# Hybrid streaming encoder step on one core: the prompt tiles' state-times-keys product moved into level 6, the output product reordered, and the gate-projection fillers dealt anew

## The chip, the cores and the metric

The kernel runs on one core of one Trainium2 chip. The metric is the device time of one execution in microseconds (us); the median of three runs is given. The engines are PE (TensorE, matrix products), DVE (VectorE), ACT (ScalarE), POOL (GpSimd) and SP (SyncE, which issues most transfers). Each works through its own instructions in the order in which they are written; between engines only semaphores order the work.

## What is computed

Two macaron layers on a residual stream of width 1024, for 512 prompt tokens and 8 sample groups of 16 tokens that share all weights. The first layer's mixer has four gated-DeltaNet heads and four mLSTM heads of size 128. The change touches the DeltaNet heads on the prompt alone:

```python
def gated_delta_chunked(q, k, v, beta, g, S0):
    ...
    A = jnp.eye(cs, dtype=jnp.float32) + jnp.where(strict, beta[..., :, None] * kk * gam, 0.0)
    eG = jnp.exp(G)
    rhs = jnp.concatenate([beta[..., None] * v, (beta * eG)[..., None] * k], axis=-1)
    sol = lax.linalg.triangular_solve(A, rhs, left_side=True, lower=True, unit_diagonal=True)
    u_v, w = sol[..., :dv], sol[..., dv:]
    p_qk = jnp.einsum('nbhtd,nbhsd->nbhts', q, k) * gam
    k_end = k * jnp.exp(G[..., -1:] - G)[..., None]
    def step(S, xs):
        q_c, u_v_c, w_c, p_c, eG_c, k_end_c, gL_c = xs
        u = u_v_c - jnp.einsum('bhtk,bhkv->bhtv', w_c, S)
        o = eG_c[..., None] * jnp.einsum('bhtk,bhkv->bhtv', q_c, S) + jnp.einsum('bhts,bhsv->bhtv', p_c, u)
        S = jnp.exp(gL_c)[..., None, None] * S + jnp.einsum('bhsk,bhsv->bhkv', k_end_c, u)
        return S, o
```

The kernel computes u as the inverse of A times (beta v minus the state times beta e^G k), so the inverse and that difference are independent of each other until the product u.

## The kernel before, in words

The program is a list of stages; the one that matters is `core`, some 170 us of the span, between the input projection and the output projection of the even mixer. It works through four prompt tiles of 128 tokens (`delta_tile`, t = 0 to 3) and then the sample tile. Nothing schedules it: the order on each engine is written out by hand. W(0) to W(8) are SBUF tiles of 128 x 4 heads x 128 floats, bank(i) is a PSUM bank, and heads(i) is the same bank seen as four heads.

A prompt tile on PE, in order: the product of keys and beta keys (`kk`); the second half of the last tile's mLSTM update (`up1`); 24 filler products; keys times queries (`np`); 4 fillers; then levels 1 to 6 of the inversion of A by doubling. A level is: two half products `m1` (two heads each), a copy of each half by ACT to W(8) (`m1c`), at level 5 a product `d2`, then two half products `d`, which DVE subtracts from W(7) (semaphore `xr`, L2838). In levels 1 to 4 DVE also transposes the half into W(6) (`x6`, L2841), and the next level's `m1` halves wait for that. At the end of each level DVE also makes the next level's mask product W(1) (`masked`, L2791, semaphore `ctl`). Between these stand parts of the mLSTM heads (`mlstm_part`) and fillers.

Behind level 6 come: `ks`, the state pS times W(0), the decayed beta keys, for which PE waits for the last `xr`; DVE's difference W(6) = v minus that (L2870, semaphore `rT`); PE's four transposes of it (L1427), ACT's copy (L2395, `rtok`), PE's product `u`, ACT's copy of it to W(1) (L2400, `utok`), and PE's output products: per head W(1) times W(5) (L1438), which waits for `utok`, and the state times q (L1439), then the state's own update and, on DVE, `keep_state`.

DVE, behind L2870, goes on with `beta_products` of the next tile (L2798 and L2580), the mLSTM denominators (L3102, a maximum of two SBUF tiles, and L3103, a reciprocal), `gate_columns`, the mLSTM output, `keep_state`, and `delta_head` of the next tile, whose product L2817 writes G_b: the first `m1` of the next tile waits for it. `kk` of the next tile waits for `gate_columns` (`expin`).

The fillers (`z_fill`, L1350) are the projection of eight weight blocks of 1024 x 128 on the tokens, 384 products of 128 x 320 in 16 halves of 24. The tables Z_FIRST, Z_HEAD, Z_D, Z_NEXT, Z_KS and Z_RT say how many stand at each place. The first product of a block waits for the low part of that block's weights (`lo_ready`), which POOL makes (L1064) after ACT's cast (`prep`, L1863). Six blocks are prepared inside the tiles: block 3, 5, 7 behind ACT's copy L2395 of tiles 0, 1, 2, and block 4, 6, 8 at level 4 of tiles 1, 2, 3. DVE also scales finished halves (`z_scale`, L2788).

```python
        Z_FIRST = 48
        Z_HEAD, Z_KS, Z_RT = 4, 8, 6
        Z_D = {1: 0, 2: 2, 3: 0, 4: 3, 5: 6, 6: 6}
        Z_NEXT = {1: 7, 2: 2, 3: 8, 4: 4, 5: 2, 6: 2}
```

Of the kernel before, what the change touches and what calls it, by code (L numbers as in the profile page):

```python
# [5 lines left out]
def stream_step(nc, ins, outs):  # L6
# [44 lines left out]
    with ctx:  # L51
# [148 lines left out]
        def bank(i):  # L200
            return ps[i // 2][:, i % 2, :]
# [69 lines left out]
        def half_at(t, l, g):  # L271

            return 2 * ((LVL - 1) * t + l - 1) + g + 1
# [21 lines left out]
        def V(i):  # L295
# [109 lines left out]
            "prod", "expin", "c0", "x0", "xt0",  # L405
            "gam", "eg",
            "kk", "np", "np_read", "tr", "ktr",
            "kend", "ctl", "x6", "xr",
            "m1", "d2", "d", "ks",
            "m1c", "rtok", "utok",  # L410
            "rT", "rt", "u", "o",
# [2 lines left out]


        Z_FIRST = 48
        Z_HEAD, Z_KS, Z_RT = 4, 8, 6
        Z_D = {1: 0, 2: 2, 3: 0, 4: 3, 5: 6, 6: 6}
        Z_NEXT = {1: 7, 2: 2, 3: 8, 4: 4, 5: 2, 6: 2}
        Z_BANK = [5, 2, 5, 5, 4, 0, 5, 4, 5, 5, 5, 4, 0, 5, 4, 5]  # L420

        def z_before(half):
# [665 lines left out]
        def _(pe):  # L1088
# [266 lines left out]
            def delta_tile(s, filled, t):  # L1355
                L = LVL
                q, k = qkv[:, 0:HA, tile(t)], qkv[:, HA:2 * HA, tile(t)]
                li, l2 = (LVL - 1) * t, (LVL - 2) * t
                if t == 0:
                    token_rows(0)  # L1360
                    z_fill(s, filled, Z_FIRST)

                pe.wait_ge(core["prod"], t + 1)

                pe.wait_ge(core["expin"], t + 1)
                per_head(4, lambda h: k[:, h], lambda h: W(0)[:, h]).then_inc(core["kk"], 1)
                if t:
                    mlstm_part(t - 1, "up1")
                z_fill(s, filled, 24)

                if t:

                    pe.wait_ge(core["up"], t)
                per_head(3, lambda h: k[:, h], lambda h: q[:, h]).then_inc(core["np"], 1)
                z_fill(s, filled, Z_HEAD)

                for l in range(1, L):
                    pe.wait_ge(core["ctl"], li + l)
                    if l == 1:

                        pe.wait_ge(core["x0"], t + 1)
                        if t % 2:

                            pe.wait_ge(z_out, Z_AT_LEVEL[t])
                    for g in range(2):
                        if l > 1:

                            pe.wait_ge(core["x6"], x6_at(t, l - 1, g))

                            pe.wait_ge(core["xr"], half_at(t, l - 1, g))  # L1390
                        c_l = G_b if l == 1 else W(1)
                        per_head(g, lambda h: c_l[:, h], lambda h: W(6)[:, h], which=TWO[g]).then_inc(core["m1"], 1)
                    if l == 1:

                        pe.wait_ge(core["xt0"], t + 1)

                        pe.wait_ge(core["np_read"], t + 1)
                        for h in range(HA):
                            last = pe.transpose(bank(3)[:, h * P:(h + 1) * P], k[:, h], ident[:])
                        last.then_inc(core["ktr"], 1)  # L1400

                    if l == 4:
                        mlstm_part(t, "kt")
                    z_fill(s, filled, Z_D[l])

                    if l < L - 1 and not quad_level(l):

                        pe.wait_ge(core["m1c"], half_at(t, l, 1))
                        per_head(2, lambda h: W(7)[:, h], lambda h: W(8)[:, h]).then_inc(core["d2"], 1)
                    for g in range(2):  # L1410

                        pe.wait_ge(core["m1c"], half_at(t, l, g))
                        per_head(g, lambda h: W(8)[:, h], lambda h: W(7)[:, h], which=TWO[g]).then_inc(core["d"], 1)

                    for part in {2: ["qk"], 3: ["vt", "kin"], 4: ["num"], 5: ["den"], 6: ["up0"]}.get(l, []):
                        mlstm_part(t, part)
                    z_fill(s, filled, Z_NEXT[l])

                pe.wait_ge(core["xr"], half_at(t, L - 1, 1))
                per_head(3, lambda h: pS[:, h], lambda h: W(0)[:, h]).then_inc(core["ks"], 1)  # L1420
                z_fill(s, filled, Z_KS)

                pe.wait_ge(core["rT"], t + 1)

                pe.wait_ge(z_out, Z_AT_RT[t])
                for h in range(HA):
                    last = pe.transpose(bank(4)[:, h * P:(h + 1) * P], W(6)[:, h], ident[:])  # L1427
                last.then_inc(core["rt"], 1)
                z_fill(s, filled, Z_RT)

                pe.wait_ge(core["rtok"], t + 1)
                per_head(3, lambda h: W(7)[:, h], lambda h: W(8)[:, h]).then_inc(core["u"], 1)

                token_rows(t + 1)

                pe.wait_ge(core["utok"], t + 1)
                for h in range(HA):
                    pe.matmul(bank(2)[:, h * P:(h + 1) * P], W(1)[:, h], W(5)[:, h], start=True, stop=False)  # L1438
                    pe.matmul(bank(2)[:, h * P:(h + 1) * P], pS[:, h], q[:, h], start=False, stop=True)  # L1439
                per_head(3, lambda h: W(3)[:, h], lambda h: W(1)[:, h]).then_inc(core["o"], 1)  # L1440
                if t == NTILE - 2:
                    mlstm_part(t, "up1")
# [396 lines left out]
        def _(act):  # L1839
# [207 lines left out]
            for s in stages:  # L2047
# [263 lines left out]
                elif kind == "core":  # L2311
# [46 lines left out]
                    for t in range(NTILE - 1):  # L2358
                        L = LVL
                        li, l2 = (LVL - 1) * t, (LVL - 2) * t  # L2360
                        decays(t)
                        if t == 0:
                            z_copy(1)
                            prep(z0 + 2)
                        z_copy([2, 5, 9, 12][t])
                        for l in range(1, L):

                            for g in range(2):

                                act.wait_ge(core["m1"], half_at(t, l, g))  # L2370
                                act.copy(two(W(8), g), two(heads(g), g)).then_inc(core["m1c"], 1)
                            for part in {2: ["gates", "qin"], 3: ["floor", "vt", "kin"], 4: ["kt"], 6: ["den"]}.get(l, []):
                                mlstm_part(t, part)
                            if l == 1:

                                act.wait_ge(core["eg"], t + 1)
                                load_beta_G(t + 1)
                                if t:

                                    act.wait_ge(ml_dve, ml(ML_DVE, t - 1, "out"))  # L2380
                                    load_floor(t)
                            z_now = {(0, 4): 3, (1, 3): 6, (1, 6): 7, (2, 4): 10, (3, 3): 13, (3, 6): 14}
                            if (t, l) in z_now:
                                z_copy(z_now[t, l])
                            if l == 4 and t < NTILE - 2:

                                act.wait_ge(ml_dve, ml(ML_DVE, t, "qk"))
                                load_gates(t + 1)
                            if l == 4 and t:
                                prep(z0 + [4, 6, 8][t - 1])  # L2390
                        if t % 2 == 0:
                            z_copy((4, 11)[t // 2])

                        act.wait_ge(core["rt"], t + 1)
                        act.copy(W(8), heads(4)).then_inc(core["rtok"], 1)  # L2395
                        if t < NTILE - 2:
                            prep(z0 + [3, 5, 7][t])

                        act.wait_ge(core["u"], t + 1)
                        act.copy(W(1), heads(3)).then_inc(core["utok"], 1)  # L2400
                        if t % 2:
                            z_copy((8, 15)[t // 2])
# [170 lines left out]
        def _(dve):  # L2573
# [277 lines left out]
            def delta_tile(t):  # L2851
# [4 lines left out]
                    beta_products(0)  # L2856
                delta_head(t)
                for l in range(1, LVL):
                    delta_level(t, l, LVL)

                    for part in {2: ["qk"], 3: ["q"]}.get(l, []):
                        mlstm_part(t, part)
                    if l == 5:
                        mul(W(0), W(0), W(2))
                        mul(q, q, W(2))
                    for half in Z_SCALE.get((t, l), []):
                        z_scale(half)

                dve.wait_ge(core["ks"], t + 1)
                own(dve.tensor_tensor(W(6), v, heads(3), ALU.subtract).then_inc(core["rT"], 1), core["rT"])  # L2870
                if t < NTILE - 2:
                    beta_products(t + 1)
                mlstm_part(t, "scale")
# [798 lines left out]
```

## Time and profile before

| what | value |
|---|---|
| median of 3 runs | 2603.61 us (2600.45 to 2605.82) |
| the profiled execution's own time | 2603.56 us |
| its span, first to last instruction | 2601.8 us |
| mean granted TensorE clock | 0.996 of full speed |
| PE busy | 2563.9 us (99%) |
| DVE busy | 2108.2 us (81%) |
| ACT busy | 1212.5 us (47%) |
| POOL busy | 355.3 us (14%) |
| prompt tiles, from the first filler to the last tile's output products | 635.1 to 806.2 us |

The profile is of one execution. What lies around its span is 1.8 us. Matrix products overlap in the array: a product's recorded time reaches past the start of the next, so the spacing of starts tells what one costs, and the idle time that a row gives counts from the end of the record, some 0.16 us after the array could have taken the next one. The clock is at its full level throughout the core stage (1.00 in all its windows).

### The profile page before, as it was taken

The page shows a single profiled execution, that of the slowest core. Times are in us where ns is not written, and L with a number is a line of the kernel's source. Part 1 is how long each engine was busy: PE and PEld are TensorE (multiplying, and loading weights), DVE is VectorE, ACT ScalarE, POOL GpSimd, SP SyncE. Part 2 cuts the span into 40 slices and gives each one's busy share as a digit, 9 for nine tenths or more (in the row PEclk, how much of TensorE's full clock was granted, in tenths as well). Part 3 has the DMA queues.
Part 4 walks back from the last instruction along what each step waited for, and adds up shares of the span by engine and source line. Part 5 has one row for each costly group of instructions (what it writes and reads, how often), then busy time and mean ns, then how long its engine had stood idle before and what let it go on. Part 6 is the DMA issues. An engine that isn't in the chain of part 4 may idle for free.

```text
span 2601.8 us, 43707 instructions
## 1 busy us (share of the span) xinstructions
PE 2563.9 (99%) x17600; PEld 2531.2 (97%) x17600; DVE 2108.2 (81%) x2614; ACT 1212.5 (47%) x1921; POOL 355.3 (14%) x186
## 2 busy tenths in 40 slices
PE   9999999999999999999999999999999999999998
PEld 9999999999999799999999999999999999999998
DVE  7979786888887789898877998987757788898756
ACT  5535454343444445454445554545311355454445
POOL 2200003232010120000023200000333300000042
PEclk9999999999999999999999999999999999999999
DMA  4223323232214422232223222322322222332231
GB/s 127 82 82 91 88 78 86 64 79 78 60 42 107 139 65 82 82 96 83 82 74 92 74 82 82 93 85 82 92 74 75 66 73 82 92 88 82 85 96 49
DMA packets 420251, 215.13 MB, mean 83 GB/s; under 512 B 19218, under 2 KB 418011, under 8 KB 420048
## 3 DMA queue, kind: packets, MB, share of 16 engines
q1 hardware_dynamic: 406066, 205.36, 27.7%
q10 hardware_dynamic: 13982, 6.96, 1.0%
q8 instruction: 140, 2.29, 0.4%
q14 instruction: 63, 0.52, 0.1%
HBM read 204.58 MB, written 7.68 MB: 82 GB/s over the span
## 4 chain that ended last, share of the span: by engine, by line
PE 83%; DVE 13%; ACT 2%; issue 1%; DMA 0%; POOL 0%; DVEq 0%; SPq 0%; ACTq 0%
PE ps L1131 16%; PE ps L1132 16%; PE ps L1133 16%; PE ps L1116 7%; PE ps L1120 7%; PE ps L1117 7%; PE ps L1326 2%; PE ps L1189 2%; PE ps L1190 2%; PE ps L1191 2%; DVE sumsq L2685 1%; DVE r L2771 1%; PE ps L1350 1%; DVE ut L2580 1%; DVE tau_lo L2649 1%
## 5 line engine op out<-in xcount | busy, mean ns | idle before, releaser
L1064 POOL TENSOR_TENSOR wlo<-raw,whi 128x1024 fp32r<-128x1024 f32 (+2 forms) x150 | 339.8, 2267 | 2208.3 <-ACT whi L1863 2208.3
L1131 PE MATMUL ps<-tau_hi,whi 128*128 128x320 f32 x1280 | 396.3, 310 | 0.5 <-ACT sq L2101 0.5
L1132 PE MATMUL ps<-tau_lo,whi 128*128 128x320 f32 x1280 | 396.0, 309 | 0.0
L1133 PE MATMUL ps<-tau_hi,wlo 128*128 128x320 f32 x1280 | 396.0, 309 | 0.0
L1874 ACT CAST whi<-raw 128x512 fp32r<-128x512 f32 (+4 forms) x368 | 258.0, 714 | 194.2 <-PE ps L1133 188.3
L1116 PE MATMUL ps<-xh,whi 128*128 128x320 f32 x1040 | 317.0, 313 | 4.3 <-POOL wlo L1064 2.3
L1117 PE MATMUL ps<-xl,whi 128*128 128x320 f32 x1040 | 313.0, 309 | 0.0
L2596 DVE TENSOR_TENSOR wlo<-raw,whi 128x512 fp32r<-128x512 f32 (+4 forms) x368 | 289.3, 800 | 17.3 <-ACT whi L1874 17.1
L1116 PE MATMUL ps<-hh,whi 128*128 128x320 f32 x928 | 281.7, 311 | 3.9 <-DVE hl L3034 1.6
L1117 PE MATMUL ps<-hl,whi 128*128 128x320 f32 x928 | 279.3, 309 | 0.0
L2596 DVE TENSOR_TENSOR wlo<-wsum,whi 128x1536 fp32r<-128x1536 f32 (+2 forms) x112 | 180.8, 1614 | 81.9 <-ACT whi L1874 80.4
L1131 PEld LDWEIGHTS ps<-tau_hi,whi 128*128 128x128 f32 x1280 | 240.8, 188 | 1.1 <-ACT sq L2101 1.0
L1132 PEld LDWEIGHTS ps<-tau_lo,whi 128*128 128x128 f32 x1280 | 240.8, 188 | 0.0
L1133 PEld LDWEIGHTS ps<-tau_hi,wlo 128*128 128x128 f32 x1280 | 240.7, 188 | 0.0
L1120 PE MATMUL ps<-xh,wlo 128*128 128x320 f32 x1040 | 236.9, 309 | 0.0
L1131 PE MATMUL ps<-xh,whi 128*128 128x320 f32 x724 | 224.2, 310 | 3.4 <-DVEq L2584 2.9
L1132 PE MATMUL ps<-xl,whi 128*128 128x320 f32 x724 | 223.8, 309 | 0.0
L1133 PE MATMUL ps<-xh,wlo 128*128 128x320 f32 x724 | 223.7, 309 | 0.0
L1131 PE MATMUL ps<-hh,whi 128*128 128x320 f32 x716 | 221.5, 309 | 0.9 <-DVEq L2584 0.6
L1132 PE MATMUL ps<-hl,whi 128*128 128x320 f32 x716 | 221.2, 309 | 0.0
L1133 PE MATMUL ps<-hh,wlo 128*128 128x320 f32 x716 | 221.1, 309 | 0.0
L1863 ACT CAST whi<-raw 128x1024 fp32r<-128x1024 f32 (+2 forms) x152 | 141.0, 929 | 160.1 <-PE ps L1120 150.6
(498 smaller groups left out, 6116.9 us busy)
## 6 DMA issues: line engine op xcount, KB each, us to landing
raw<-in_ffn_w_gu SPq DMA_DIRECT2D x320, 256.0 KB, 3.7
raw<-in_ffn_w_d SPq DMA_DIRECT2D x96, 192.0 KB, 3.0
raw<-in_w_in_even SPq DMA_DIRECT2D x32, 512.0 KB, 4.1
raw<-in_ffn_w_d SPq DMA_DIRECT2D x32, 384.0 KB, 3.6
raw<-in_w_in_odd SPq DMA_DIRECT2D x24, 512.0 KB, 3.8
raw<-in_ffn_w_gu SPq DMA_DIRECT2D x16, 512.0 KB, 4.1
raw<-in_ffn_w_d SPq DMA_DIRECT2D x64, 128.0 KB, 2.6
raw<-in_w_ple_gate SPq DMA_DIRECT2D x16, 512.0 KB, 4.0
```

What stands on the lines that cost most here:

```text
L1064: pool.tensor_tensor(ring(wlo, n), raw[:, slot, 0:kt, :], ring(whi, n).bitcast(fp32), ALU.subtract).then_inc(lo_ready, 1)
L1116: pe.matmul(ps[j % 4][:, c, 0:HT], wh[:, k], hi[:, k, cs], start=(k == 0), stop=False)
L1117: pe.matmul(ps[j % 4][:, c, 0:HT], wh[:, k], lo[:, k, cs], start=False, stop=False)
L1120: last = pe.matmul(ps[j % 4][:, c, 0:HT], wl[:, k], hi[:, k, cs], start=False, stop=(k == kt - 1))
L1131: pe.matmul(out, whi[:, w], hi(i), start=(start and i == 0), stop=False, skip_group_check=True)
L1132: pe.matmul(out, whi[:, w], lo(i), start=False, stop=False, skip_group_check=True)
L1133: last = pe.matmul(out, wlo[:, w], hi(i), start=False, stop=(i == kt - 1), skip_group_check=True)
L1189: pe.matmul(out, whi[:, w], high[:, k, cs], start=(start and k == ks[0]), stop=False, skip_group_check=True)
L1190: pe.matmul(out, whi[:, w], low[:, k, cs], start=False, stop=False, skip_group_check=True)
L1863: act.copy(ring(whi, n), raw[:, raw_pos["block", n], 0:kt, :]).then_inc(hi_ready, 1)
L1874: act.copy(group_ring(whi, p, g), group_raw(p, g)).then_inc(pair_hi, 1)
L2596: dve.tensor_tensor(group_ring(wlo, p, g), group_raw(p, g), group_ring(whi, p, g).bitcast(fp32), ALU.subtract).then_inc(pair_lo, 1)
```

## The change

In the prompt tiles, and there alone: `ks` moves from behind level 6 to the middle of level 6, behind its `m1` halves, and waits for a new semaphore `kdec`, which DVE's decayed beta keys give at level 5. DVE's difference (`rT`) moves ahead of level 6's subtractions. PE's transposes of it follow level 6's `d` at once, the mLSTM part `up0` stands behind them, and one run of 12 fillers in the place of two of 8 and 6. ACT's copy of the transposes goes to W(4), which is free by then, and not to W(8). The state-times-q products stand ahead of the wait for `utok`. Of the fillers behind the `m1` of level 6 there were 22 a tile (6, 2, 8 and 6) and are 12; of the 10 others, three stand at the end of level 1, two pairs between the `m1` halves of levels 2 and 3, one behind the `m1` of level 4, and one at each of the two places of level 5. There are 384 as before, and no other instruction is added or dropped.

```diff
-            "kend", "ctl", "x6", "xr",
+            "kdec", "ctl", "x6", "xr",
...
-        Z_HEAD, Z_KS, Z_RT = 4, 8, 6
-        Z_D = {1: 0, 2: 2, 3: 0, 4: 3, 5: 6, 6: 6}
-        Z_NEXT = {1: 7, 2: 2, 3: 8, 4: 4, 5: 2, 6: 2}
+        Z_HEAD, Z_RT = 4, 12
+        Z_PAIR = {2: 2, 3: 2}
+        Z_D = {1: 0, 2: 2, 3: 0, 4: 4, 5: 7, 6: 0}
+        Z_NEXT = {1: 10, 2: 2, 3: 8, 4: 4, 5: 3}
...
                     for g in range(2):
+                        if g:
+                            z_fill(s, filled, Z_PAIR.get(l, 0))
...
+                    if l == L - 1:
+
+                        pe.wait_ge(core["kdec"], t + 1)
+                        per_head(3, lambda h: pS[:, h], lambda h: W(0)[:, h]).then_inc(core["ks"], 1)
                     z_fill(s, filled, Z_D[l])
...
-                    for part in {2: ["qk"], 3: ["vt", "kin"], 4: ["num"], 5: ["den"], 6: ["up0"]}.get(l, []):
+                    for part in {2: ["qk"], 3: ["vt", "kin"], 4: ["num"], 5: ["den"]}.get(l, []):
                         mlstm_part(t, part)
-                    z_fill(s, filled, Z_NEXT[l])
-
-                pe.wait_ge(core["xr"], half_at(t, L - 1, 1))
-                per_head(3, lambda h: pS[:, h], lambda h: W(0)[:, h]).then_inc(core["ks"], 1)
-                z_fill(s, filled, Z_KS)
+                    if l < L - 1:
+                        z_fill(s, filled, Z_NEXT[l])
...
                 last.then_inc(core["rt"], 1)
+                mlstm_part(t, "up0")
+
+                pe.wait_ge(core["xr"], half_at(t, L - 1, 1))
                 z_fill(s, filled, Z_RT)
 
                 pe.wait_ge(core["rtok"], t + 1)
-                per_head(3, lambda h: W(7)[:, h], lambda h: W(8)[:, h]).then_inc(core["u"], 1)
+                per_head(3, lambda h: W(7)[:, h], lambda h: W(4)[:, h]).then_inc(core["u"], 1)
 
                 token_rows(t + 1)
+
+                for h in range(HA):
+                    pe.matmul(bank(2)[:, h * P:(h + 1) * P], pS[:, h], q[:, h], start=(h == 0), stop=False, skip_group_check=True)
 
                 pe.wait_ge(core["utok"], t + 1)
                 for h in range(HA):
-                    pe.matmul(bank(2)[:, h * P:(h + 1) * P], W(1)[:, h], W(5)[:, h], start=True, stop=False)
-                    pe.matmul(bank(2)[:, h * P:(h + 1) * P], pS[:, h], q[:, h], start=False, stop=True)
+                    pe.matmul(bank(2)[:, h * P:(h + 1) * P], W(1)[:, h], W(5)[:, h], start=False, stop=(h == HA - 1), skip_group_check=True)
...
-                        act.copy(W(8), heads(4)).then_inc(core["rtok"], 1)
+                        act.copy(W(4), heads(4)).then_inc(core["rtok"], 1)
...
                 for l in range(1, LVL):
+                    if l == LVL - 1:
+
+                        dve.wait_ge(core["ks"], t + 1)
+                        own(dve.tensor_tensor(W(6), v, heads(3), ALU.subtract).then_inc(core["rT"], 1), core["rT"])
                     delta_level(t, l, LVL)
...
                     if l == 5:
-                        mul(W(0), W(0), W(2))
+                        own(dve.tensor_tensor(W(0), W(0), W(2), ALU.mult).then_inc(core["kdec"], 1), core["kdec"])
                         mul(q, q, W(2))
...
-                dve.wait_ge(core["ks"], t + 1)
-                own(dve.tensor_tensor(W(6), v, heads(3), ALU.subtract).then_inc(core["rT"], 1), core["rT"])
```

The order on DVE around level 6 (the end of level 5 is the product W_92<-W_92; L2838, in the change L2847, are the two subtractions of level 6; L2870, in the change L2871, is the difference; L2798, in the change L2807, is the first beta product). Before:

```order
L2580 TENSOR_TENSOR W_92<-W_92 128x512 [waits core_xr]
L2580 TENSOR_TENSOR qkv<-qkv,W_92 128x4x128 [waits dve_own]
L2788 TENSOR_TENSOR qkv<-qkv,r 128x4x80 [waits z_out,dve_own]
L2838 TENSOR_TENSOR W_92<-W_92,ps 128x256 [waits core_d,z_scaled]
L2838 TENSOR_TENSOR W_92<-W_92,ps 128x256 [waits core_d,core_xr]
L2870 TENSOR_TENSOR W_92<-qkv,ps 128x512 [waits core_ks,core_xr]
L2798 TENSOR_TENSOR W_92<-qkv,beta_b 128x512 [waits beta_G_loaded,core_rT]
L2580 TENSOR_TENSOR qkv<-qkv,beta_b 128x4x128 [waits core_prod]
L3102 TENSOR_TENSOR V_79<-V_79 128x512 [waits ml_act,dve_own]
```

And in the change:

```order
L2877 TENSOR_TENSOR W_92<-W_92 128x512 [waits core_xr]
L2589 TENSOR_TENSOR qkv<-qkv,W_92 128x4x128 [waits core_kdec]
L2797 TENSOR_TENSOR qkv<-qkv,r 128x4x80 [waits z_out,dve_own]
L2871 TENSOR_TENSOR W_92<-qkv,ps 128x512 [waits core_ks,z_scaled]
L2847 TENSOR_TENSOR W_92<-W_92,ps 128x256 [waits core_d,core_rT]
L2847 TENSOR_TENSOR W_92<-W_92,ps 128x256 [waits core_d,core_xr]
L2807 TENSOR_TENSOR W_92<-qkv,beta_b 128x512 [waits beta_G_loaded,core_xr]
L2589 TENSOR_TENSOR qkv<-qkv,beta_b 128x4x128 [waits core_prod]
L3113 TENSOR_TENSOR V_79<-V_79 128x512 [waits ml_act,dve_own]
```

The difference stands ahead of level 6's two subtractions and not behind them; all else keeps its place.

The order on PE in tile 1, level 4, behind the mLSTM part `num` (the pairs L1690 and L1691, in the change L1699 and L1700), where four fillers stand ahead of level 5's first `m1` half. Before:

```order
L1691 MATMUL ps<-qkv,pC 128x128
L1350 MATMUL ps<-xh,wlo 128x320
L1350 MATMUL ps<-xh,whi 128x320
L1350 MATMUL ps<-xl,whi 128x320
L1350 MATMUL ps<-xh,wlo 128x320
L1326 MATMUL ps<-W_92 128x128 [waits core_xr,core_x6,core_ctl]
```

And in the change:

```order
L1700 MATMUL ps<-qkv,pC 128x128
L1351 MATMUL ps<-xl,whi 128x320
L1351 MATMUL ps<-xh,wlo 128x320
L1351 MATMUL ps<-xh,whi 128x320 [waits z_out,lo_ready]
L1351 MATMUL ps<-xl,whi 128x320
L1327 MATMUL ps<-W_92 128x128 [waits core_xr,core_x6,core_ctl]
```

The first filler of block 4, with its wait for the block's low part, stood one level later, behind the mLSTM part `den` of level 5, and is now the third of these four.

The order on PE from the middle of level 6 on, in the change (L1327 with pS is `ks`, the next four rows' products of W_92 are `d`, L1431 are the transposes, L1673 is `up0`):

```order
L1327 MATMUL ps<-W_92,pS 128x128 [waits core_kdec]
L1327 MATMUL ps<-W_92,pS 128x128 x3
L1327 MATMUL ps<-W_92 128x128 [waits core_m1c]
L1327 MATMUL ps<-W_92 128x128
L1327 MATMUL ps<-W_92 128x128 [waits core_m1c]
L1327 MATMUL ps<-W_92 128x128
L1431 MATMUL ps<-ident,W_92 128x128 [waits z_out,core_rT]
L1431 MATMUL ps<-ident,W_92 128x128 x3
L1673 MATMUL ps<-V_79 128x129 [waits ml_act]
L1673 MATMUL ps<-V_79 128x129
L1351 MATMUL ps<-xh,whi 128x320 [waits core_xr]
```

Before, six fillers stood between `m1` and `d`, two more and `up0` between `d` and `ks`, and eight between `ks` and the transposes; no filler stands between any of these now.

## Rows read from the trace of the kernel before

**Rows 1.** The page: each engine's busy time, share of the span, instructions.
```profile
PE 2563.9 (99%) x17600; PEld 2531.2 (97%) x17600; DVE 2108.2 (81%) x2614; ACT 1212.5 (47%) x1921; POOL 355.3 (14%) x186
```
**Rows 2.** PE's waits, 630 to 803 us: total us, times, longest us.
```profile
PE ps L1326 <- DVE W L2841: 2.9, 11, 0.4
PE ps L1438 <- ACT W L2400: 1.7, 3, 0.6
```
**Rows 3.** Busy time, one stretch: length; PE, PEld, DVE, ACT, POOL busy; clock, DMA.
```profile
717.17:730.42 13.25, 12.68 (x100) 12.15 (x98) 12.63 (x19) 6.21 (x13) 2.35 (x1) 1.00 0.13 40
```
**Rows 4.** Timeline of PE from tile 1's level 6 (start us, us, operation).
```profile
712.48 1.05 PE L1326 MATMUL ps<-W 128*128 128x128 f32 x8
...
714.25 1.05 PE L1326 MATMUL ps<-W 128*128 128x128 f32 x8
715.14 0.61 PE L1664 MATMUL ps<-V 128*128 128x129 f32 x4
...
715.90 1.16 PE L1326 MATMUL ps<-W,pS 128*128 128x128 f32 x8
...
718.06 0.60 PE L1427 MATMUL ps<-ident,W 128*128 128x128 f32 x4
...
720.33 0.27 PE L1331 MATMUL ps<-ident,R 128*128 128x128 f32 x1
721.17 0.49 PE L1438 MATMUL ps<-W 128*128 128x128 f32 x2 [0.57 <-ACT W L2400]
```
**Rows 5.** Timeline of DVE, the same stretch.
```profile
714.97 0.88 DVE L2838 TENSOR_TENSOR W<-W,ps 128x256 f32<-128x256 f32 x2 [1.53 <-PE ps L1326]
717.17 0.69 DVE L2870 TENSOR_TENSOR W<-qkv,ps 128x512 f32<-128x512 f32 x1 [1.32 <-PE ps L1326]
717.89 0.69 DVE L2798 TENSOR_TENSOR W<-qkv,beta_b 128x512 f32<-128x512 f32 x1
...
719.34 0.69 DVE L3102 TENSOR_TENSOR V<-V 128x512 f32<-128x512 f32 x1
...
729.67 0.69 DVE L2817 TENSOR_TENSOR G_b<-W,level 128x512 f32<-128x512 f32 x1
```
**Rows 6.** Timeline of PE, level 2 of tile 0, levels 2 and 3 of tile 1.
```profile
652.42 0.68 PE L1326 MATMUL ps<-W 128*128 128x128 f32 x4
653.31 0.71 PE L1326 MATMUL ps<-W 128*128 128x128 f32 x4 [0.20 <-DVE W L2841]
...
693.38 0.68 PE L1326 MATMUL ps<-W 128*128 128x128 f32 x4 [0.42 <-DVE W L2841]
694.27 0.71 PE L1326 MATMUL ps<-W 128*128 128x128 f32 x4 [0.20 <-DVE W L2841]
```
**Rows 7.** Timeline of PE, tile 1, fillers behind level 4.
```profile
706.40 0.31 PE L1350 MATMUL ps<-xh,whi 128*128 128x320 f32 x1
706.55 0.31 PE L1350 MATMUL ps<-xl,whi 128*128 128x320 f32 x1
```
**Rows 8.** Timeline of POOL, then of DVE, tiles 0 and 1.
```profile
645.90 2.52 POOL L1064 TENSOR_TENSOR wlo<-raw,whi 128x1024 fp32r<-128x1024 f32 x1 [14.83 <-ACT whi L1863]
...
705.79 2.37 POOL L1064 TENSOR_TENSOR wlo<-raw,whi 128x1024 fp32r<-128x1024 f32 x1 [24.08 <-ACT whi L1863]
720.30 2.35 POOL L1064 TENSOR_TENSOR wlo<-raw,whi 128x1024 fp32r<-128x1024 f32 x1 [12.14 <-ACT whi L1863]
...
645.49 0.69 DVE L2813 TENSOR_TENSOR W<-ident,W 128x512 f32<-128x512 f32 x1
706.16 2.88 DVE L2788 TENSOR_TENSOR qkv<-qkv,r 128x320 f32<-128x320 f32 x2
```
**Rows 9.** DVE line L2788, one form: duration ns min/median/max.
```profile
L2788 DVE TENSOR_TENSOR qcopy<-qcopy,r x2: 493/493/493, 662.0 to 665.2; 128x320 f32<-128x320 f32 x2
```
**Rows 10.** Timeline of ACT, tile 1's copy of the transposes, and the cast.
```profile
718.70 0.59 ACT L2395 COPY W<-ps 128x512 f32<-128x512 f32 x1 [3.94 <-PE ps L1427]
719.18 1.05 ACT L1863 CAST whi<-raw 128x1024 fp32r<-128x1024 f32 x1
```

## The prediction

> **What bounds the kernel now.** I read the page first: PE is busy for 99% of the span, DVE for 81% [rows 1], so time can only come from gaps in PE's work, or from the chain that makes them. The change touches the core stage alone. There PE's list of waits names two that it could end: 2.9 us in 11 waits for transposed halves of the levels, and 1.7 us in 3 waits for ACT's copy of u [rows 2]; with the fourth tile's, of the same length, the latter is 4 waits. But the records overlap, so I go by starts. Eight passes cost 0.89 us (714.25 to 715.14), a single transpose pass thus 0.11, and the output products start at 721.17 where they could at 720.44: 0.73 us a tile [rows 4]. A filler costs 0.15 [rows 7].
>
> The stretches by engine then show what PE's view does not. From the difference L2870 of tile 1 to the first product of tile 2's level 1, DVE is busy 12.63 of 13.25 us with 19 instructions, and the rest is 0.03 between one and the next [rows 3]. The last of them, G_b, ends at 730.36, and PE's level 1 starts at 730.42 [rows 3, 5]. So behind the difference DVE sets the pace, not the copy of u: whatever PE saves there it loses again at level 1. What counts is how long after the start of level 6 DVE reaches its beta products. Now that is 717.89 minus 712.48, or 5.41 us, with DVE idle for 1.53 and 1.32 us in it [rows 4, 5].
>
> **The change, part by part.**
>
> *State times keys and difference within level 6.* Level 6's m1 takes 0.89. ks starts behind it; its semaphore kdec does not hold it up: the decayed keys come right behind level 5's last subtraction, for which m1 itself has waited, and take 0.69 as their like do [rows 5], less than m1's 0.89. From its start to DVE's difference it is 1.27 us now (715.90 to 717.17), of which 0.10 is the slower start behind a wait (1.16 against 1.05 us for eight passes) that goes: 1.17 [rows 4, 5]. The difference and its step are 0.72, the two subtractions 0.91 [rows 5], and their d products, 0.89 of PE, are done while the difference runs. So beta products start 0.89 + 1.17 + 0.72 + 0.91 = 3.69 after level 6, which is 1.72 us sooner. PE's transposes wait for the difference some 0.1 us, without cover, but PE is then ahead of DVE.
>
> *Fillers dealt anew.* Ten fillers a tile move ahead of level 6. Three at the end of level 1 fall into the gap before 693.38 (0.42 us of idle by the record, 0.56 by starts), two each into the gaps between the halves of levels 2 and 3 (0.20 by the record, 0.44 by starts) [rows 2, 6]. They cost nothing where DVE's transposes are what PE waits for. The three others, in levels 4 and 5, where PE has no gap, put level 6 off by 3 x 0.147 = 0.44. In tile 0 level 2 began without a wait at 652.42; 3 fillers, half a product and 2 fillers later is 0.44 + 0.45 + 0.29 behind that, 653.60 against 653.31: 0.3 more there [rows 6].
>
> *Fillers at level 4 of tile 1.* The third filler there is the first of block 4, and waits for POOL's low part. POOL runs it from 705.79 to 708.16 [rows 8]. That filler would come at 706.55 plus 0.15 [rows 7], so PE stands for 1.46 us and a handover of 0.05 (as from 730.36 to 730.42): 1.5. PE has no gap from there to level 6, so all of it reaches ks. No other tile has such a wait: block 6 begins at the 12 fillers behind tile 2's level 6, block 8 is not in the tiles.
>
> *State products ahead of utok.* Eight passes, 0.89, stand now in the gap of 0.73 [rows 4]. The gap goes four times, but the next wait is late in its place: kk will wait for gate_columns some 0.3 us, and level 1 for G_b another 0.2 to 0.3, since PE has 10 fillers (1.47) and 0.73 less behind level 6, 2.2 in all, while DVE is only 1.72 earlier. I count nothing beyond DVE's 1.72.
>
> *Copy to W(4), up0 and scaling.* The same lengths; ACT and the sample tile's state loads (issued behind DVE's last mLSTM update) move with DVE. Nothing.
>
> **The sum.** Per tile 1.72 - 0.44 = 1.28. Tile 0: 1.28 - 0.3 = 1.0. Tile 1: 1.28 - 1.5 = -0.2. Tiles 2 and 3: 1.28 each. In all 3.4 us. Against the profiled execution's own 2603.56 that is 2600.2; it lies 0.05 below the median of the runs, which makes no difference.
>
> **A price the trace shows only elsewhere.** DVE's scaling of 128 x 320 takes 0.49 us [rows 9]. The pair that starts at 706.16, 0.37 us after POOL's operation, takes 2.88 [rows 8]: without its own 2 x 0.49 and 0.04 the first stood still until 708.03, which is 0.13 before POOL's record ends. So POOL can shut DVE out of an operation that reads two SBUF tiles. The maximum L3102 is one. Now it starts 2.17 behind the difference's start and POOL 3.13 (717.17 to 720.30), beneath the reciprocal, which is not disturbed [rows 5, 8]. In the change the maximum comes at 2.17 + 0.91 = 3.08. POOL comes at 0.69 + 0.05 (transposes), + 0.64 + 0.05 (copy, behind a wait), + 0.48 and 1.12 (cast, POOL) = 3.03 [rows 4, 9, 10]. That is a tie. The nearest row for it: at 645.90 POOL's record begins while DVE's two-tile operation of 645.49 runs to 646.18, and becomes 2.52 instead of 2.36 long, 0.16 more where 0.28 were left [rows 8]. So POOL seems to ask 0.12 after its record begins, at 3.15 here, and the maximum is first by 0.07. I take nothing for it; the ends are 0 and 2.2 us in each of tiles 0 to 2.
>
> The Trainium skill (SBUF — State Buffer, section "SBUF: two separate sides") says that a VectorE operation with two SBUF inputs and a GpSimd operation that reads SBUF exclude each other for a whole instruction, whoever starts first. The trace agrees at 706.16 (2.39 us for 0.49). By the records' starts alone that rule would let POOL win here, and the sum would be rival 1's.
>
> **The rivals.**
>
> 1. *POOL is first* in tiles 0, 1 and 2. The maximum then stands until 0.13 before POOL's end: 3.03 + 2.36 - 0.13 - 3.08 = 2.2 us, three times 6.6 us, all on DVE's chain. 2600.2 + 6.6 = 2606.8, slower than before. It decides at a lead of POOL's request over the maximum of 0.0 us; its starts are 0.05 ahead, its request by my reading 0.07 behind.
> 2. *PE's gaps are the bound* and DVE has hidden room, or block 4 does not have to wait. Then each gap filled counts: 4 x 0.73, 3 x 0.44 (level 2's first half) and 8 x 0.29 (the pairs) = 6.6 us, 2597.0. DVE's 12.63 of 13.25 speaks against it.
> 3. *Part of it.* POOL wins in one tile or two, or the uncovered wait for the difference grows by some tenths: 2601.5 to 2604.5, which cannot be told from no change.
>
> **How the numbers follow.** My forecast has 0.52, rival 1 0.22, rival 2 0.13, rival 3 0.13. The runs before spread by 0.2% (2600.45 to 2605.82), and 0.2%, 5.2 us, is about what a measurement can tell from no change. The bounds for that are 2598.4 and 2608.8. The forecast lies 1.8 above the lower one and the runs' own spread is as large, so a quarter of its chance and most of rival 2's is called faster: 0.22. Slower needs rival 1 and 2 us more: 0.06. The rest, 0.72, is no change. The range reaches from near rival 2 to rival 1: 2597.4 to 2607.2.
>
> **What would show it.** Right: no wait left before the W(1) output products; new waits of 0.2 to 0.4 us before kk and before level 1 in tiles 1 to 3; DVE idle once, for about 1.5 us or less, before the difference, and not before the subtractions; one wait of PE for POOL of 1.5 us in tile 1's level 4; tiles 2 and 3 each 1.3 us shorter and tile 1 about as long; clock unchanged. Wrong: a maximum of 2.9 us (rival 1); prompt tiles shorter by 6 us (rival 2); no wait for POOL (that step).

## The result, and the profile after

The changed kernel takes 2605.71 us (median of 20 runs, 2604.69 to 2613.15) against 2601.04 us for the kernel before (20 runs, 2600.01 to 2605.83), a ratio of 1.0019 with a 95% interval of 1.0013 to 1.0025. It is slower by 4.7 us, where 3.4 us less was forecast. The profiled execution took 2605.55 us, with a span of 2603.7. Two of the 35 executions of the kernel before that stand beside the first four experiments lasted 4686 and 5475 us, and no median or ratio below counts them.

I begin with PE's waits in the prompt tiles of the changed kernel (630 to 803 us; total us, times, longest us):

```profile
PE ps L1327 <- DVE gcols L2813: 7.2, 3, 2.4
...
PE ps L1351 <- POOL wlo L1065: 1.0, 1, 1.0
PE ps L1327 <- DVE G_b L2826: 0.7, 1, 0.7
```

Both waits of [rows 2] are gone, as intended: the transposed halves (2.9 us) and the copy of u (1.7). Larger than the two together is a wait of kk for `gate_columns`, three times 2.4 us. I had expected it at 0.3. DVE's timeline around level 6 of tile 1 tells why (start us, us, operation, idle before it):

```profile
718.44 0.69 DVE L2871 TENSOR_TENSOR W<-qkv,ps 128x512 f32<-128x512 f32 x1 [1.30 <-PE ps L1327]
719.16 0.88 DVE L2847 TENSOR_TENSOR W<-W,ps 128x256 f32<-128x256 f32 x2
720.07 0.69 DVE L2807 TENSOR_TENSOR W<-qkv,beta_b 128x512 f32<-128x512 f32 x1
720.79 0.69 DVE L2589 TENSOR_TENSOR qkv<-qkv,beta_b 128x512 f32<-128x512 f32 x1
721.52 2.87 DVE L3113 TENSOR_TENSOR V<-V 128x512 f32<-128x512 f32 x1
724.42 3.35 DVE L3114 RECIPROCAL V<-V 128x512 f32<-128x512 f32 x1
727.81 0.23 DVE L2813 COPY gcols<-ps 128x68 f32<-128x68 f32 x1
```

The stage itself came out as planned. DVE is idle once, for 1.30 us, before the difference, and not before the subtractions, where [rows 5] had 1.53 and 1.32. But the maximum (L3113, L3102 before) is 2.87 us long and not 0.69. POOL's timeline has the other half of it, in tiles 0 to 2:

```profile
677.23 2.36 POOL L1065 TENSOR_TENSOR wlo<-raw,whi 128x1024 fp32r<-128x1024 f32 x1 [28.77 <-ACT whi L1872]
...
721.48 2.36 POOL L1065 TENSOR_TENSOR wlo<-raw,whi 128x1024 fp32r<-128x1024 f32 x1 [11.48 <-ACT whi L1872]
...
764.42 2.36 POOL L1065 TENSOR_TENSOR wlo<-raw,whi 128x1024 fp32r<-128x1024 f32 x1 [9.83 <-ACT whi L1872]
```

The three long ones among the maxima stand right behind them:

```profile
677.26 2.88 DVE L3113 TENSOR_TENSOR V<-V 128x512 f32<-128x512 f32 x1
...
764.45 2.87 DVE L3113 TENSOR_TENSOR V<-V 128x512 f32<-128x512 f32 x1
```

POOL's record begins 0.03 us before the maximum's in tiles 0 and 2, 0.04 in tile 1, and each time the maximum stands for about 2.18 us: in tile 0, 677.23 + 2.36 - 0.13 + 0.69 = 680.15, and it ends at 680.14. In tile 3, where there is no POOL operation, it is 0.69. The start of the difference to the maximum is 3.08 us and to POOL 3.04 in tile 1 (worked out: 3.08 and 3.03). That is rival 1 in its own numbers. By the Trainium skill (SBUF — State Buffer, section "SBUF: two separate sides"), whoever starts first has the shared port for the whole instruction; the trace agrees, down to a lead of 0.03 us.

A second cost was in no case of mine. Windows of the changed kernel behind the three waits of 2.4 us, which stand before the kk that follows tiles 0, 1 and 2 (length; PE, PEld, DVE, ACT, POOL busy; clock, DMA):

```profile
685.50:688.80 3.30, 3.30 (x14) 3.30 (x14) 3.09 (x7) 1.91 (x5) 0.00 (x0) 0.53 0.00 0
729.70:733.20 3.50, 3.50 (x16) 3.50 (x16) 3.29 (x7) 1.96 (x5) 0.00 (x0) 0.53 0.00 0
772.50:776.00 3.50, 3.50 (x26) 3.50 (x26) 3.21 (x7) 2.41 (x6) 0.00 (x0) 1.00 0.01 2
```

After the first two stands of 2.4 us the granted clock fell to about its lower level (1.2 of 2.4 GHz), and after the third it did not. Before, the same fillers of tile 1 ran at 1.00:

```profile
726.30:729.80 3.50, 3.50 (x28) 3.50 (x27) 3.29 (x7) 1.83 (x5) 0.00 (x0) 1.00 0.00 0
```

PE's timeline of the changed kernel shows it in the spacing, 0.27 us from filler to filler where [rows 7] has 0.15, until 732.83:

```profile
728.18 1.13 PE L1327 MATMUL ps<-W,qkv 128*128 128x128 f32 x8 [2.40 <-DVE gcols L2813]
...
730.97 0.47 PE L1351 MATMUL ps<-xh,wlo 128*128 128x320 f32 x1
731.23 0.47 PE L1351 MATMUL ps<-xh,whi 128*128 128x320 f32 x1
```

PE is then late for level 1, and the next DVE operation waits for it, 1.12 us behind the first stand and here, behind the second, 1.11:

```profile
735.82 0.69 DVE L2829 TENSOR_TENSOR W<-ps,W 128x512 f32<-128x512 f32 x1 [1.11 <-PE ps L1327]
```

**The ledger by tile.** The beta product marks each tile on DVE's chain, and the sample tile's marks their end. Before:

```profile
676.93 0.69 DVE L2798 TENSOR_TENSOR W<-qkv,beta_b 128x512 f32<-128x512 f32 x1
...
758.84 0.69 DVE L2798 TENSOR_TENSOR W<-qkv,beta_b 128x512 f32<-128x512 f32 x1
...
806.19 0.69 DVE L2908 TENSOR_TENSOR W<-qkv,beta_b 128x512 f32<-128x512 f32 x1
```

and after, with 720.07 above for tile 1 (717.89 in [rows 5]):

```profile
675.81 0.69 DVE L2807 TENSOR_TENSOR W<-qkv,beta_b 128x512 f32<-128x512 f32 x1
...
763.00 0.69 DVE L2807 TENSOR_TENSOR W<-qkv,beta_b 128x512 f32<-128x512 f32 x1
...
811.01 0.69 DVE L2919 TENSOR_TENSOR W<-qkv,beta_b 128x512 f32<-128x512 f32 x1
```

The differences are -1.12, +2.18, +4.16 and +4.82: tile by tile -1.1, +3.3, +2.0, +0.7. A maximum falls behind its tile's mark and so counts in the next. To line up the kernels I take all marks from POOL's first record of the prompt tiles: from 645.90 before [rows 8] to 806.19 are 160.29 us, after it is 645.93 to 811.01, 165.08. This *stretch* grew by 4.8 us, and the medians by 4.7. The spans of the two profiles differ by only 1.9 (2601.8, 2603.7), for a reason that lies behind the prompt tiles: in the profile of before the clock fell in the sample tile. (So it was at its full level in the prompt tiles, and not, as said ahead of the forecast, throughout the core stage.) Before, then two runs of the experiments below (e1, e4):

```profile
850.00:855.00 5.00, 5.00 (x23) 4.48 (x22) 1.23 (x1) 1.24 (x4) 0.00 (x0) 0.50 0.00 0
```
```profile
850.00:855.00 5.00, 4.75 (x51) 4.27 (x50) 4.84 (x5) 3.50 (x9) 1.75 (x1) 1.00 0.00 0
```
```profile
845.00:850.00 5.00, 5.00 (x26) 4.05 (x25) 2.38 (x3) 1.86 (x4) 0.39 (x1) 0.76 0.00 0
```

Why it comes in some profiles and not in others is open. So below each experiment is read by its stretch, which ends ahead of it, beside its median.

### The profile page after: what moved, and what is told of

Read it like the earlier page. It is cut to its first block, busy times and chain, and to the rows that moved or that the text cites. A ratio compares the mean times of both kernels' runs of the same rounds, so it can differ in the third digit from the quotient of the medians.

```text
span 2603.7 us, 43707 instructions
## 1 busy us (share of the span) xinstructions
PE 2562.3 (98%) x17600; PEld 2532.9 (97%) x17600; DVE 2112.6 (81%) x2614; ACT 1212.8 (47%) x1921; POOL 355.6 (14%) x186
## 4 chain that ended last, share of the span: by engine, by line
PE 56%; DVE 8%; ACT 2%; issue 1%; POOL 0%; DVEq 0%; ACTq 0%
PE ps L1132 13%; PE ps L1134 13%; PE ps L1133 13%; PE ps L1117 5%; PE ps L1121 5%; PE ps L1118 5%; PE ps L1190 1%; PE ps L1192 1%; PE ps L1191 1%; DVE sumsq L2694 1%; DVE ut L2589 1%; DVE x L3416 1%; DVE tau_lo L2658 1%; DVE r L2780 0%; DVE x L3601 0%
```

## The experiments

My theory: the change is worth what the forecast said, and loses it, and more, to POOL's lead of 0.03 us. Two rivals from the forecast are open, that gaps of PE count by themselves (rival 2), and that the stall of the maximum is not the whole loss. Results:

| run | median us | ratio to before (95%) | stretch us, against before's 160.29 |
|---|---|---|---|
| the change | 2605.71 | 1.0019 (1.0013 to 1.0025) | 165.08, +4.8 |
| e1 cast behind the copy of u | 2597.00 | 0.9982 (0.9974 to 0.9991) | 156.42, -3.9 |
| e2 state products alone | 2600.66 | 0.9998 (0.9990 to 1.0007) | 160.06, -0.2 |
| e3 PE kept busy in the stand | 2603.45 | 1.0008 (0.9999 to 1.0016) | 162.91, +2.6 |
| e4 both casts behind the copy of u | 2596.26 | 0.9978 (0.9970 to 0.9987) | 155.10, -5.2 |
| e5 e1's edit in the kernel before | 2602.68 | 1.0002 (0.9993 to 1.0011) | 160.29, 0.0 |
| e6 e1 without the state products' move | 2598.52 | 0.9986 (0.9977 to 0.9995) | 157.49, -2.8 |
| e7 a small copy ahead of the cast | 2597.12 | 0.9976 (0.9966 to 0.9985) | 156.39, -3.9 |

The kernel before had 2601.75 us (33 runs) beside e1 to e4, and 2601.37 (25 runs) beside e5 to e7. A median is of 9 to 12 runs of each experiment, the stretch of one.

**e1: POOL out of the maximum's way.** ACT casts block 3, 5 or 7 behind its copy of u, so POOL comes beneath the reciprocal, as before the change.

```
-                        if t < NTILE - 2:
-                            prep(z0 + [3, 5, 7][t])

                         act.wait_ge(core["u"], t + 1)
                         act.copy(W(1), heads(3)).then_inc(core["utok"], 1)
+                        if t < NTILE - 2:
+                            prep(z0 + [3, 5, 7][t])
```

> The changed kernel, with ACT's cast of weight blocks 3, 5 and 7 issued behind its copy of u and not behind its copy of the transposes, so that POOL's operation starts some 3 us later, beneath the reciprocal. Theory (POOL shuts DVE out of the maximum): the maximum takes 0.69 us in tiles 0 to 2 instead of 2.88, the wait before kk falls from 2.4 to some 0.2 us, the granted clock stays full; 2605.7 - 3 x 2.2 - 1.5 (what the slower clock cost) = 2597.6, that is 3.4 us under before. Rival (the new order of products or the fillers cost the time, POOL is only nearby): 2605 or more, the wait before kk stays.

POOL starts at 721.43 in tile 1 and the maximum takes 0.69 us. PE's waits of e1, as above:

```profile
PE ps L1351 <- POOL wlo L1065: 1.1, 1, 1.1
PE ps L1327 <- DVE G_b L2826: 0.7, 1, 0.7
PE ps L1327 <- DVE gcols L2813: 0.7, 3, 0.2
```

The clock stays up, and the beta products stand at:

```profile
675.84 0.69 DVE L2807 TENSOR_TENSOR W<-qkv,beta_b 128x512 f32<-128x512 f32 x1
716.85 0.69 DVE L2807 TENSOR_TENSOR W<-qkv,beta_b 128x512 f32<-128x512 f32 x1
756.51 0.69 DVE L2807 TENSOR_TENSOR W<-qkv,beta_b 128x512 f32<-128x512 f32 x1
802.35 0.69 DVE L2919 TENSOR_TENSOR W<-qkv,beta_b 128x512 f32<-128x512 f32 x1
```

Tile by tile that is -1.1, +0.1, -1.3 and -1.5 against before; the forecast had -1.0, +0.2, -1.3 and -1.3. The rest of the change does what was worked out, and the whole loss goes when POOL's operation falls elsewhere.

**e5: the same edit without the change.** It asks whether the cast's place is worth something by itself. The diff is that of e1, in the kernel before.

> The kernel before the change, with ACT's cast of blocks 3, 5 and 7 moved behind its copy of u (the control for e1, where the same edit in the changed kernel gave 2597.0). Theory: the cast's new place is worth nothing by itself, it only keeps POOL away from the maximum, and in the kernel before the maximum L3102 (0.69 us) is never disturbed. POOL goes from 720.30 to about 721.4, where DVE's operations with a PSUM input run, DVE's chain keeps its length, and the time stays within 1 us of the kernel before: 2601.9 in the last comparison, so 2601 to 2602. Rival: ACT gives u's copy 1.1 us sooner, and the output products behind it, so that the gap of 0.73 us before them closes and PE gains it in three tiles: 2599.7.

The stretch is the same to 0.01 us and the interval of the ratio holds 1, so it is worth nothing. POOL came at 722.31 in tile 1, not at 721.4, 2.08 us into the reciprocal of 3.35, and the maximum kept its 0.69. The copy of u comes no sooner: PE's wait for it is still 1.7 us in 3 times.

**e7: who is first, and nothing else.** The cast stays where the change has it, with one copy ahead of it that nothing reads.

```
                         if t < NTILE - 2:
+                            act.copy(W(8)[:, 0], ident[:])
                             prep(z0 + [3, 5, 7][t])
```

> The changed kernel with one more small ACT copy ahead of the cast (the identity, 128 x 128, into a part of W(8) that nothing reads then), so that the cast and POOL's operation come about 0.2 us later and nothing else moves. Theory: in the changed kernel POOL's record begins only 0.03 to 0.04 us before the maximum's, and the first of the two holds the other off to its end. 0.2 us later the maximum (0.69 us) is first, POOL's own record becomes about 0.5 us longer (2.36 to 2.9), PE does not stand before kk, its granted clock stays 1.00, and the time is that of e1, 2597 to 2598. Rival (POOL's size or place, not who is first, makes the stall): the maximum stays at 2.7 to 2.9 us and the time at 2605.7.

The copy put the cast off by 0.20 us. DVE and POOL in tile 1 of e7:

```profile
718.28 0.69 DVE L3114 TENSOR_TENSOR V<-V 128x512 f32<-128x512 f32 x1
```
```profile
718.45 2.75 POOL L1065 TENSOR_TENSOR wlo<-raw,whi 128x1024 fp32r<-128x1024 f32 x1 [11.69 <-ACT whi L1872]
```

The maximum is first by 0.17 us and takes 0.69; now POOL is the one that waits, 2.75 us instead of 2.36 (I had expected 2.9), at no cost; so it is in tiles 0 and 2. With one operation more the kernel is 8.6 us faster than the change (2597.12 against 2605.71, from two series). The two traces bracket the point that decides: with POOL's record 0.03 to 0.04 ahead POOL has the port, with the maximum's 0.17 ahead DVE has it. POOL's record overlaps the maximum's for 0.52 us (718.45 to 718.97) and grows by 0.39, so 0.13 of the overlap is not waited for, where the forecast had 0.12 from [rows 8]. A record's length alone does not tell whether those 0.13 lie at its start (a late request) or at the other's end (an early release).

**e3: the price of the clock.** In tiles 1 to 3, 18 transposes whose result nothing reads stand before kk, so PE is busy for 2.0 of the 2.4 us of the stand; the maximum stays long.

```
+                if t:
+                    unused_products(bank(1)[:, 0:P], 18)
                 pe.wait_ge(core["prod"], t + 1)
```

> The changed kernel with 18 transposes of the identity into unused columns of PSUM (2.0 us of PE) ahead of PE's wait for kk in tiles 1 to 3; their result is read by nothing. Theory (the stand of 2.4 us took the clock down to half, and the slow fillers behind it made PE late for level 1): granted clock 1.0 behind kk, fillers 0.147 us apart and not 0.267, DVE's idle of 1.1 us before the np product goes; about 1.9 us faster than the changed kernel, 2603.8. Rival (the slow stretch is hidden behind DVE, or the clock has another cause): same time or slower.

The same fillers of tiles 0 and 1 in e3 run at the upper level:

```profile
685.50:688.80 3.30, 3.30 (x25) 3.30 (x24) 3.09 (x7) 2.27 (x6) 0.00 (x0) 1.00 0.00 0
728.60:732.10 3.50, 3.50 (x27) 3.50 (x26) 3.29 (x7) 2.02 (x5) 0.00 (x0) 1.00 0.02 5
```

The stretch is 2.2 us shorter than the change's, as is the median (2603.45 against 2605.71, from different series), and the maxima are still 2.87 to 2.88 us. So of the 8.7 us between the change and e1, 2.2 are the slower clock behind two stands (DVE's two waits of 1.12 and 1.11 us) and 6.5 (162.91 - 156.42) are DVE's stall itself, for which the forecast had 6.6.

**e2: the state products alone**, in the kernel before.

```
+                for h in range(HA):
+                    pe.matmul(bank(2)[:, h * P:(h + 1) * P], pS[:, h], q[:, h], start=(h == 0), stop=False, skip_group_check=True)
+
                 pe.wait_ge(core["utok"], t + 1)
                 for h in range(HA):
-                    pe.matmul(bank(2)[:, h * P:(h + 1) * P], W(1)[:, h], W(5)[:, h], start=True, stop=False)
-                    pe.matmul(bank(2)[:, h * P:(h + 1) * P], pS[:, h], q[:, h], start=False, stop=True)
+                    pe.matmul(bank(2)[:, h * P:(h + 1) * P], W(1)[:, h], W(5)[:, h], start=False, stop=(h == HA - 1), skip_group_check=True)
```

> The kernel before with one part of the change alone: the four state-times-q products stand ahead of the wait for ACT's copy of u. Theory (DVE's chain from the difference to level 1 sets the pace): the gap of 0.73 us before the output products goes, and comes back as a wait before kk and before level 1; time within 0.7 us of before. Rival (PE's gaps set the pace): 4 x 0.73 = 2.9 us faster.

PE's waits of e2:

```profile
PE ps L1326 <- DVE W L2843: 2.9, 11, 0.4
PE ps L1326 <- DVE gcols L2806: 1.6, 3, 0.5
```

The wait for u's copy (1.7 us in 3 times) became one for `gate_columns` (1.6 in 3), and the stretch gained 0.2 us where four gaps of 0.73 closed. In the kernel before, DVE is the bound of this piece and not PE, against rival 2.

**e6: the same move undone in e1**, where DVE's chain is shorter.

```
-                for h in range(HA):
-                    pe.matmul(bank(2)[:, h * P:(h + 1) * P], pS[:, h], q[:, h], start=(h == 0), stop=False, skip_group_check=True)
-
...
-                    pe.matmul(bank(2)[:, h * P:(h + 1) * P], W(1)[:, h], W(5)[:, h], start=False, stop=(h == HA - 1), skip_group_check=True)
+                    pe.matmul(bank(2)[:, h * P:(h + 1) * P], W(1)[:, h], W(5)[:, h], start=True, stop=False)
+                    pe.matmul(bank(2)[:, h * P:(h + 1) * P], pS[:, h], q[:, h], start=False, stop=True)
```

> e1 (the changed kernel with the cast of blocks 3, 5 and 7 behind the copy of u) with the output products in the order of before: each head's W(1) product ahead of its state product, both behind the wait for the copy of u. Theory: DVE is the bound of the tile. PE stands some 0.5 us before the output products again, but of that about 0.2 (the wait for gate_columns before kk) and 0.2 (the wait for G_b before level 1) are waits that shrink instead, so 0.1 to 0.2 us a tile: 2597.0 becomes 2597.4 to 2597.8. Rival (each gap of PE counts): 4 x 0.73 = 2.9 us, 2599.9.

The stretch is 1.1 us longer than e1's: more than my 0.4 to 0.8 and less than the rival's 2.9. The medians cannot tell these apart (the intervals of their ratios are 4 to 5 us wide). PE's waits, and DVE in tile 2:

```profile
PE ps L1445 <- ACT W L2405: 2.3, 4, 0.6
```
```profile
766.69 0.69 DVE L2587 TENSOR_TENSOR W<-ps,W 128x512 f32<-128x512 f32 x1 [0.67 <-ACT W L2352]
```

In e1 DVE does not wait there (765.44, 0.10 behind the operation before). With the gap back, kk is late, ACT's exponents with it, and DVE waits 0.67 us for them. So with the difference moved ahead, PE and DVE are nearly level: the move is worth 0.2 us alone and 1.1 on top of the rest.

**e4: the other cast too.** In e1, blocks 4, 6 and 8 were still cast at level 4, where block 4's low part comes late. Here both casts of a tile stand behind the copy of u.

```
-                            if l == 4 and t:
-                                prep(z0 + [4, 6, 8][t - 1])
...
                         if t < NTILE - 2:
                             prep(z0 + [3, 5, 7][t])
+                            prep(z0 + [4, 6, 8][t])
```

> As e1_cast_behind_u, and the cast of blocks 4, 6 and 8 follows at once at the same place, in tiles 0 to 2, instead of at level 4 of tiles 1 to 3. Theory: PE's wait for POOL in tile 1's level 4 (1.2 us) goes, and DVE's scalings of 2.4 us at level 4 become 0.5; since PE is then the bound of levels 2 to 6 only the first counts, so 1.2 to 1.5 us faster than e1: 2596.2. Rival A: DVE's freed 1.9 us per tile count too, 6 us faster than e1. Rival B: POOL's second operation shuts DVE out of the head of the next tile (W(4) times mask) and takes it back, no faster than e1.

POOL's timeline has its operations in pairs, and the wait for the low part is gone from PE's list:

```profile
680.32 4.74 POOL L1065 TENSOR_TENSOR wlo<-raw,whi 128x1024 fp32r<-128x1024 f32 x2 [31.95 <-ACT whi L1872]
720.01 4.74 POOL L1065 TENSOR_TENSOR wlo<-raw,whi 128x1024 fp32r<-128x1024 f32 x2 [34.95 <-ACT whi L1872]
```

Its stretch is 1.3 us shorter than e1's. The medians show 0.7 of it, within their scatter; its profile has the sample tile's slower clock shown above and e1's has not. Neither 6 us more than e1 (rival A) nor nothing (rival B) came of it. It has the lowest median of all; the interval of its ratio lies below 1, as those of e1, e6 and e7 do, and the change's above.

## Why the prediction was wrong

**The step that failed** is the last of the working: "POOL seems to ask 0.12 after its record begins, at 3.15 here, and the maximum is first by 0.07. I take nothing for it". The times of the records were right: worked out 0.05 ahead, measured 0.03 and 0.04. Wrong was to move POOL's start by 0.12 and leave the maximum's where it was. The same rows held the like figure for DVE: where DVE is the one that waits, its stall too is shorter than the overlap of the records. Two more rows of the kernel before show it:

```profile
746.92 2.37 POOL L1064 TENSOR_TENSOR wlo<-raw,whi 128x1024 fp32r<-128x1024 f32 x1 [24.27 <-ACT whi L1863]
```
```profile
747.12 2.52 DVE L2788 TENSOR_TENSOR qkv<-qkv,r 128x320 f32<-128x320 f32 x1
```

The overlap is 2.17 us and the stall 2.52 - 0.49 = 2.03, or 0.14 less. It is 0.14 at 706.16 too (the first of that pair takes 2.35 us; the 2.39 of the forecast holds the step of 0.04), and 0.14 in the changed kernel, whose maxima overlap POOL for 2.32 to 2.33 us and stand for 2.18 to 2.19. For POOL the figure is 0.12 to 0.14 (645.90; e7). I had booked it as a late request for POOL and as an early release for DVE. Read the same way for both, it leaves the order of the records as it is, and POOL is first, as it was in all three tiles. Which of the two ways is the true one no run here shows; that a lead of 0.03 by the records decides is measured. So the bare order of like records was the better guide, and the rule of the Trainium skill (SBUF — State Buffer, section "SBUF: two separate sides"), read by those, was right. Above all, a tie at a price of 6.6 us was given a chance of 0.22 on the costly side, when the record starts spoke for it, and nothing of that price went into the sum.

**Rival 1's price** was right for what it held: 2.18 us each against 2.2, and 6.5 us in all against 6.6. It left out what PE does during the stand. The stalls became PE's waits, and the clock took 2.2 us more. Rival 1 alone gave 6.6 - 3.4 = 3.2 us more than before; with the clock's 2.2, and 0.5 by which the other terms were better, that is 4.9, where the stretch has 4.8. That 2605.71 lies between 2597.4 and 2607.2 is luck: the range was built on a profiled execution of 2603.56, and the kernel before has a median of 2601.04 in the comparison. As a difference the range went from -6.2 to +3.6, and +4.7 is outside it. The chance of slower, 0.06, was set as if rival 1 could bring no more than its own 6.6.

**The sum of the terms** was right, as e1 shows: -3.4 forecast, -3.9 measured. By its steps:
- State times keys, the difference and the fillers (1.28 a tile): tile 2 gained 1.3, tile 3 gained 1.5.
- Tile 0, 1.0 forecast, was 1.1.
- The wait for block 4's low part: 1.5 forecast, 1.04 by the record and 1.2 by starts (708.71 plus 0.15 to 710.06). The forecast left POOL's start where it was before, 0.91 us ahead of the filler's; POOL came at 707.65, 1.21 ahead of it. Tile 1 lost 0.1 instead of 0.2, and e4 won 1.3 by taking the wait away.
- "The gap goes four times, but the next wait is late in its place": shown by e2. kk's wait in e1 is 0.2 by the record, 0.3 forecast; level 1's wait for G_b is 0.18 by starts in tile 1 (688.04 plus 0.15 to 688.37), 0.2 to 0.3 forecast, and too short for PE's list, whose 0.7 is tile 0's.
- "I count nothing beyond DVE's 1.72" held only as part of the whole: e6 puts 1.1 us on this move.

**Rivals 2 and 3.** e1 stands at -3.9 and not at -6.6, and e2 gained 0.2 and not 2.9. Rival 3 was not it, since POOL was first in all three tiles.

## What to carry to other kernels

When a step moves an operation that reads two SBUF tiles on DVE, look for what POOL does within some tenths of its new place, and keep them apart on purpose: here the place of one line was worth 8.7 us, and a copy that puts POOL off by 0.2 us and does nothing else was worth as much. When two starts come out as a tie, compare like with like, and give the costly side its half of the chance. And price a new stand of PE with the fillers behind it, not by its length alone.

## What was not expected of the hardware

- Two of three stands of 2.4 us on PE, in an otherwise full stretch, were followed by 3.3 and 3.5 us at a granted clock of 0.53. Keeping PE busy for 2.0 of the 2.4 us (e3) kept it at 1.00. Why the third stand had no such sequel stays open.
- A lead of 0.03 us by the records' starts gave POOL the port in three tiles of three (and three of three in e3), each time for a DVE stall of 2.18 to 2.19 us. The other way round the stall is short: POOL stood 0.39 us.
- In the profiles of the kernel before and of e5 the sample tile ran at 0.50 from 850 to 855 us, though from 835 to 860 PE waited no more than 0.4 us at a time; in those of the change, e1, e2, e3, e6 and e7 it stayed at 1.00, and in e4's it was 0.76 from 845 to 850. It is worth some 2.7 us: e2's span is 2598.9 against 2601.8, with a stretch only 0.2 shorter. That is as much as the effects studied here, so the stretches ahead of it were compared. Its cause was not tried.
